# Gated attention of a two-block model: decayed scores and values split for three of four key blocks, products one step later

## The chip, the cores and the metric

One core of one Trainium2 chip. The metric is the device time of one execution in microseconds (us), the median of the runs of a kernel. One execution was also recorded by the hardware profiler; its rows are in microseconds unless marked ns.

## The reference

The model is two transformer blocks over 512 tokens of width 1024. The change lies in the first block's gated attention (4 heads of 128), which the reference computes in chunks with a running state. Cut to one chunk:

```python
sc = jnp.einsum('bhtd,bhsd->bhts', qc, kc) * jnp.exp(dmat - m_t[..., None])
...
num = (jnp.einsum('bhts,bhse->bhte', sc, vc)
       + w_inter[..., None] * jnp.einsum('bhtd,bhde->bhte', qc, C))
den = sc.sum(axis=-1) + w_inter * jnp.einsum('bhtd,bhd->bht', qc, n)
h = num / jnp.maximum(jnp.abs(den), jnp.exp(-m_t))[..., None]
```

Behind it come a norm over each head, `hb * rsqrt(mean(hb * hb) + eps)`, a gain and a gate `sigmoid(ob)`.

## The kernel before

**Number format.** Where the kernel wants accuracy and speed, it splits an f32 tile x into a high part (x copied to F32R) and a low part (x minus the high part) and multiplies in three F32R passes, `split_mm` (L471 to L475): high by high, high by low, low by high. Where it does not split, it multiplies f32 by f32 in one instruction pair, which TensorE runs more slowly.

**Weights.** They stream through a ring of three slots: the SP queue loads a unit (128 x 1024), ScalarE makes `w_hi` (`feed`, L1122), GpSimd makes `w_lo` (`low_part`, L417), TensorE multiplies. A unit of a gate is one output tile of 512 tokens over 8 inner tiles, so 24 passes of 512 columns. `quarter(name, q)` issues a quarter of a unit (6 passes), and the code puts quarters between the steps of an attention so that TensorE has work while the other engines prepare.

**The gated attention.** The whole of it is computed as one masked product over 512 tokens, key block by key block (i = 0 to 3, of 128 keys). Only queries from i * 128 on see block i, so its width is 512, 384, 256 and 128 columns. For each head h and block i:
- ScalarE makes the decay (`decay`, L1363 and L1365: Relu, then Exp) in `em[i % 2]`.
- TensorE makes the scores S (L797) in bank 2 or 3.
- VectorE masks the diagonal part of the decay (L2056) and multiplies scores by decay into `em[2 + i % 2]` (L2060); this frees the bank and counts `ml_sc`.
- TensorE multiplies the values (L806, bank 4) and ones (L807, bank 5: the denominators) by that tile, summing over the blocks, and counts `ml_nd`. Both are f32. These are called P0 to P3 below.

Then VectorE finishes the head: a copy of a gate tile (L1861), two operations on the denominators (L2074, L2075), a reciprocal (L2078) and the multiply L2079; ScalarE squares the result (L1438), TensorE sums the squares (`mean_square`, L786), ScalarE takes the norm (`head_rms`, L1410 and L1413), VectorE applies it (`head_y`, L2039 and L2041), ScalarE and VectorE split it (`head_out` L1417, `head_low` L2046).

**The order of the work is written out by hand** for each engine. Before the change TensorE's order in head h is: quarter 0, S0, quarter 1, the squares' sum of head h-1, S1, P0, quarter 2, S2, P1, quarter 3, S3, P2, quarter 4, P3, quarters 5, 6, 7. VectorE has, for block i, the mask and the multiply, and puts `head_y(h-1)` behind block 1 and `head_low(h-1)` behind block 2 (in head 0 the last rotary tile, `rope(7)`, behind block 1). ScalarE has in head h: a feed of a weight unit, `head_rms(h-1)`, decay 2, `head_out(h-1)`, decay 3, a feed, an Exp for the floor of the denominator, decays 0 and 1 of head h+1, and the square. Ahead of head 0, ScalarE has the eighth copy of the rotary stage (L1393) with four DMA issues (L1398).

Behind the four heads stands the next attention (`softmax_attention`, scores L654), whose first softmax on VectorE is queued behind the last head's L2079.

Of the kernel before, what the change touches and what calls it, by code (L numbers as in the profile page):

```python
# [20 lines left out]
F32 = mybir.dt.float32  # L21
F32R = mybir.dt.float32r
# [4 lines left out]
P = 128  # L27
T = 512
# [88 lines left out]
def build(nc, stream, xT, memT, vecs, tabs, relb, outT):  # L117
    with ExitStack() as ctx, ExitStack() as work:
# [69 lines left out]
        em = [ar(f"em{i}", [P, T], F32, 72 + 2 * i) for i in range(4)]  # L188
        mprobs = [ar(f"mprobs{i}", [P, T], F32, 56 + 2 * i) for i in range(4)]
# [270 lines left out]
        def _(pe):  # L460
# [261 lines left out]
            def first_unit(j, order):  # L722

                for k2, i in order:
# [6 lines left out]
                    pe.wait_ge(named("first_lo"), k + 1)  # L731
# [56 lines left out]
            for h in range(NHB):  # L788
                quarter("gate1a", 8 * h)
                for i in range(QT + 1):  # L790
                    if i < QT:
                        b = 2 + i % 2
                        acquire(b)
                        if h == 0 and i == 0:
                            pe.wait_ge(named("qkb_done"), 8)
                            pe.wait_ge(named("vb_copied"), 4)
                        pe.matmul(ps[:, b, 0:T - i * P], qkb[:, 4 + h, i * P:i * P + P], qkb[:, h, i * P:T],  # L797
                                  start=True, stop=True).then_inc(named("ml_s"), 1)
                    if i >= 1:
                        j = i - 1  # L800
                        if j == 0:
                            acquire(4)
                            acquire(5)
                        pe.wait_ge(named("ml_sc"), QT * h + i)
                        x = em[2 + j % 2][:, 0:T - j * P]
                        pe.matmul(ps[:, 4, j * P:T], vb[:, j, h * P:h * P + P], x, start=j == 0, stop=j == QT - 1)  # L806
                        pe.matmul(ps[:, 5, j * P:T], ones, x, start=j == 0, stop=j == QT - 1)\  # L807
                          .then_inc(named("ml_nd"), 1)
                    if i < QT:
                        quarter("gate1a", 8 * h + 1 + i)  # L810
                    if i == 0 and h >= 1:
                        mean_square(h - 1)
                for q in range(QT + 1, 8):
                    quarter("gate1a", 8 * h + q)
# [292 lines left out]
        def _(act):  # L1107
# [151 lines left out]
            def first_raw(k):  # L1259

                if f"x{k}" in loads:
                    act.wait_ge(loads[f"x{k}"], 16)
                act.activation(first_hi[:, k], hT[:, k], ACT.Copy, scale=vec[:, VEC["mix"] + k:VEC["mix"] + k + 1])\
                   .then_inc(named("first_hi"), 1)
# [142 lines left out]

            def head_rms(h):
# [10 lines left out]
            for h in range(NHB):  # L1419
                feed_after(FIRST["gate1a"] + 2 * h)  # L1420
                if h >= 1:
                    head_rms(h - 1)
                decay(h, 2)
                if h >= 1:
                    head_out(h - 1)
                decay(h, 3)
# [385 lines left out]
        def _(dve):  # L1812
# [107 lines left out]
            def first_low(k):  # L1920

                dve.wait_ge(named("first_hi"), k + 1)
                dve.scalar_tensor_tensor(out=first_lo[:, k], in0=hT[:, k], scalar=v("mix", k),
                                         in1=first_hi[:, k].bitcast(F32), op0=ALU.mult, op1=ALU.subtract)\
                   .then_inc(named("first_lo"), 1)
# [109 lines left out]

            def head_y(h):
# [12 lines left out]
            for h in range(NHB):  # L2049
                for i in range(QT):  # L2050
# [7 lines left out]
                    if QT * h + i >= 2:  # L2058
                        dve.wait_ge(named("ml_nd"), QT * h + i - 1)
# [3 lines left out]

                    if i == 1 and h >= 1:
                        head_y(h - 1)
# [570 lines left out]
```

## Time and profile before

| | |
|---|---|
| median of 3 runs | 1717.01 us (1716.93 to 1717.64) |
| profiled execution, its own time | 1717.28 us |
| its span | 1715.5 us |
| TensorE busy | 1702.6 us (99%) |
| VectorE, ScalarE, GpSimd busy | 859.4, 650.1, 657.6 us |
| granted TensorE clock | 0.999 |
| w_lo on GpSimd (L417) | x261, mean 2471 ns |
| w_hi on ScalarE (L1122) | x272, mean 1055 ns |

The span runs from the first to the last recorded instruction; the profiled execution's own time is 1.8 us longer. A matmul's record covers its whole way through the array and overlaps the next one, so its price is read from start to start. An f32 matmul leaves two records, each with a weight load of its own.

### The profile page before, as it was taken

What the parts mean: (1) busy time and instruction counts of PE and PEld (TensorE: products, weight loads), DVE (VectorE), ACT (ScalarE), POOL (GpSimd) and SP (SyncE); (2) the same over time, 40 slices, a digit from 0 to 9 for tenths busy, and PEclk for the clock granted to TensorE, in tenths of its full rate; (3) what the DMA queues carried; (4) which work ended last, traced back from release to release, by engine and by line L of the source; (5) the groups of instructions that cost most, each with busy time, mean ns of one, the idle gap of its engine ahead of it and who ended that gap; (6) DMA issues with size and microseconds to landing.
All of it is one profiled execution on the core that took longest, in us unless ns stands there. A gap on an engine that the chain in (4) does not pass through costs nothing.

```text
span 1715.5 us, 23737 instructions
## 1 busy us (share of the span) xinstructions
PE 1702.6 (99%) x8133; PEld 1362.2 (79%) x8133; DVE 859.4 (50%) x1398; ACT 650.1 (38%) x1076; POOL 657.6 (38%) x276
## 2 busy tenths in 40 slices
PE   9999999999999999999999999999999999999998
PEld 6888676788888888888688766778888988888887
DVE  5733665574655552208387675551333775555013
ACT  6333444534222222327433576452223522222122
POOL 2443322244544444444333100224444344444443
PEclk9999999999999999999999999999999999999999
DMA  5354211223332333224422111122333233333331
GB/s 188 105 190 129 92 62 50 74 74 123 111 98 94 92 96 104 90 99 129 145 85 88 37 50 45 55 59 93 95 98 98 84 101 98 98 95 93 105 96 64
DMA packets 47635, 162.29 MB, mean 95 GB/s; under 512 B 5724, under 2 KB 7900, under 8 KB 47304
## 3 DMA queue, kind: packets, MB, share of 16 engines
q1 hardware_dynamic: 43872, 151.10, 27.9%
q10 hardware_dynamic: 3688, 10.20, 1.9%
q8 instruction: 46, 0.75, 0.2%
q14 instruction: 29, 0.24, 0.0%
HBM read 156.91 MB, written 4.76 MB: 94 GB/s over the span
## 4 chain that ended last, share of the span: by engine, by line
PE 94%; DVE 2%; ACT 1%; issue 1%; DMA 1%; ACTq 0%; SPq 0%; DVEq 0%
PE ps L473 27%; PE ps L475 27%; PE ps L474 27%; PE ps L672 2%; PE ps L654 2%; PE ps L1052 1%; PE ps L1051 1%; PE ps L1053 1%; PE ps L698 1%; PE ps L911 1%; PE ps L952 1%; PE ps L881 1%; PE ps L933 1%; DVE tmp L1825 1%; PE ps L680 0%
## 5 line engine op out<-in xcount | busy, mean ns | idle before, releaser
L417 POOL TENSOR_TENSOR w_lo<-w_raw,w_hi 128x1024 fp32r<-128x1024 f32 x261 | 644.5, 2471 | 1038.5 <-ACT w_hi L1122 1011.6
L473 PE MATMUL ps<-u_hi,w_hi 128*128 128x512 f32 x1352 | 545.8, 404 | 0.2
L475 PE MATMUL ps<-u_hi,w_lo 128*128 128x512 f32 x1352 | 527.5, 390 | 0.0
L474 PE MATMUL ps<-u_lo,w_hi 128*128 128x512 f32 x1352 | 526.7, 390 | 0.0
L1122 ACT ACTIVATE w_hi<-w_raw 128x1024 fp32r<-128x1024 f32 x272 | 286.6, 1055 | 398.8 <-PE ps L475 331.8
L473 PEld LDWEIGHTS ps<-u_hi,w_hi 128*128 128x128 f32 x1352 | 254.0, 188 | 61.1 <-issue 10.6
L475 PEld LDWEIGHTS ps<-u_hi,w_lo 128*128 128x128 f32 x1352 | 253.7, 188 | 53.8
L474 PEld LDWEIGHTS ps<-u_lo,w_hi 128*128 128x128 f32 x1352 | 254.3, 188 | 51.6 <-issue 2.4
L1519 ACT ACTIVATE tmp<-tmp 128x512 f32<-128x512 f32 x44 | 27.8, 632 | 213.2 <-DVEq L2169 213.2
L2179 DVE TENSOR_TENSOR a_lo<-tmp,a_hi 128x512 f32 (+1 forms) x44 | 105.3, 2392 | 5.6 <-DVE a_hi L2178 1.6
L473 PE MATMUL ps<-a_hi,w_hi 128*128 (+1 forms) x264 | 102.9, 390 | 0.0
L475 PE MATMUL ps<-a_hi,w_lo 128*128 (+1 forms) x264 | 102.7, 389 | 0.0
L474 PE MATMUL ps<-a_lo,w_hi 128*128 (+1 forms) x264 | 102.7, 389 | 0.0
L2175 DVE TENSOR_TENSOR tmp<-ps,tmp 128x512 f32<-128x512 f32 x44 | 30.4, 692 | 91.5 <-PE ps L475 91.2
L2167 DVE TENSOR_TENSOR tmp<-ps,tmp 128x512 f32<-128x512 f32 x44 | 30.4, 692 | 58.6 <-PE ps L475 45.0
L473 PEld LDWEIGHTS ps<-a_hi,w_hi 128*128 128x128 f32 x264 | 49.6, 188 | 10.5
L475 PEld LDWEIGHTS ps<-a_hi,w_lo 128*128 128x128 f32 x264 | 49.6, 188 | 10.4
L474 PEld LDWEIGHTS ps<-a_lo,w_hi 128*128 128x128 f32 x264 | 49.6, 188 | 10.1
L2136 DVE TENSOR_TENSOR tmp<-ps,tmp 128x512 f32<-128x512 f32 x16 | 11.1, 692 | 91.1 <-PE ps L475 90.0
L473 PE MATMUL ps<-m_hi,w_hi 128*128 128x512 f32 (+1 forms) x152 | 54.3, 357 | 0.0
L475 PE MATMUL ps<-m_hi,w_lo 128*128 128x512 f32 (+1 forms) x152 | 54.1, 356 | 0.0
L474 PE MATMUL ps<-m_lo,w_hi 128*128 128x512 f32 (+1 forms) x152 | 54.0, 356 | 0.0
(373 smaller groups left out, 2398.1 us busy)
## 6 DMA issues: line engine op xcount, KB each, us to landing
w_raw<-stream SPq DMA_DIRECT2D x277, 512.0 KB, 3.5
g_rep<-g_one ACTq DMA_DIRECT2D x1, 2560.0 KB, 13.8
spread<-m_rows ACTq DMA_DIRECT2D x4, 512.0 KB, 5.0
tmp<-tmp ACTq DMA_DIRECT2D x32, 64.0 KB, 3.3
bias<-g_rep ACTq DMA_DIRECT2D x1, 2048.0 KB, 10.4
outT<-hT SPq DMA_DIRECT2D x16, 128.0 KB, 1.8
hT<-xT SPq DMA_DIRECT2D x3, 512.0 KB, 7.9
mem_in<-memT ACTq DMA_DIRECT2D x1, 1024.0 KB, 4.7
```

The costliest lines, as they stand in the source:

```text
L417: pool.tensor_tensor(w_lo[:, slot], w_raw[:, slot], w_hi[:, slot].bitcast(F32), ALU.subtract)\
L473: pe.matmul(out, wh, xh, start=start, stop=False)
L474: pe.matmul(out, wh, xl, start=False, stop=False)
L475: return pe.matmul(out, wl, xh, start=False, stop=stop)
L654: m = pe.matmul(ps[:, 2 + e, 0:keys[t]], head_q(h, t), head_k(h, keys[t]), start=True, stop=not extra(t))
L672: m = pe.matmul(ps[p0:p1, b, t * P:t * P + P], values(h, kb), prT[e][:, kb * P:kb * P + P], start=kb == 0, stop=kb == nb - 1)
L698: m = pe.transpose(ps[:, 4 + e, kb * P:kb * P + P], pr[s % 4][:, kb * P:kb * P + P], ident)
L1122: act.activation(w_hi[:, slot], w_raw[:, slot], ACT.Copy).then_inc(hi_ready, 1)
L1519: act.activation(tmp[0][:, :], tmp[1][:, :], ACT.Sigmoid).then_inc(named(name + "_e"), 1)
L2167: step(dve.tensor_tensor(tmp[1][:, :], ps[:, banks[0], :], tmp[3][:, :], ALU.mult))
L2175: step(dve.tensor_tensor(tmp[4][:, :], ps[:, banks[1], :], tmp[2][:, :], ALU.mult))
L2179: step(dve.tensor_tensor(a_lo[:, bass.ds(k, 1)], a, a_hi[:, bass.ds(k, 1)].bitcast(F32), ALU.subtract))
```

## The change

The decayed scores of blocks 0 to 2 are copied to a high part by ScalarE (`em_high`) and the low part is made by VectorE (`em_low`). The values of key blocks 0 to 2 are split once for all heads (`vb_hi` on ScalarE, `vb_lo` on VectorE, written over the f32 values), and ScalarE makes an F32R copy of the ones. For these blocks TensorE issues three F32R passes for the values and two for the ones; block 3 stays f32. In the loop over steps, the products of block j come at step j + 2, not j + 1, so P0 stands behind S2, P3 behind quarter 5, and quarters 6 and 7 are left behind it. `em_low(h, i-1)` stands on VectorE behind the multiply of block i. On ScalarE, `head_rms` and `head_out` come behind `em_high` of blocks 0 and 1. The semaphores `first_hi` and `first_lo` get other names and count these parts too.

```diff
@@ -186,6 +186,11 @@
         g1b = [ar(f"g1b{k}", [P, T], F32, 40 + 2 * k) for k in range(KT)]
         rows = ar("rows", [4, 8, T], F32, 56)
         em = [ar(f"em{i}", [P, T], F32, 72 + 2 * i) for i in range(4)]
+        vb_hi = ar("vb_hi", [P, QT - 1, T], F32R, 56)
+        vb_lo = ar("vb_lo", [P, QT - 1, T], F32R, 40)
+        em_hi = [ar(f"em_hi{i}", [P, T], F32R, 64 + 2 * i) for i in range(2)]
+        em_lo = [ar(f"em_lo{i}", [P, T], F32R, 68 + 2 * i) for i in range(2)]
+        ones_r = ar("ones_r", [P, P], F32R, 88)
         mprobs = [ar(f"mprobs{i}", [P, T], F32, 56 + 2 * i) for i in range(4)]
         mprobsT = [ar(f"mprobsT{i}", [P, T], F32, 64 + 2 * i) for i in range(2)]
         cos = ar("cos", [P, T], F32, 90)
@@ -787,31 +792,37 @@
 
             for h in range(NHB):
                 quarter("gate1a", 8 * h)
-                for i in range(QT + 1):
+                for i in range(QT + 2):
                     if i < QT:
                         b = 2 + i % 2
                         acquire(b)
                         if h == 0 and i == 0:
                             pe.wait_ge(named("qkb_done"), 8)
-                            pe.wait_ge(named("vb_copied"), 4)
                         pe.matmul(ps[:, b, 0:T - i * P], qkb[:, 4 + h, i * P:i * P + P], qkb[:, h, i * P:T],
                                   start=True, stop=True).then_inc(named("ml_s"), 1)
-                    if i >= 1:
-                        j = i - 1
+                    if i >= 2:
+                        j = i - 2
                         if j == 0:
                             acquire(4)
                             acquire(5)
-                        pe.wait_ge(named("ml_sc"), QT * h + i)
-                        x = em[2 + j % 2][:, 0:T - j * P]
-                        pe.matmul(ps[:, 4, j * P:T], vb[:, j, h * P:h * P + P], x, start=j == 0, stop=j == QT - 1)
-                        pe.matmul(ps[:, 5, j * P:T], ones, x, start=j == 0, stop=j == QT - 1)\
-                          .then_inc(named("ml_nd"), 1)
-                    if i < QT:
-                        quarter("gate1a", 8 * h + 1 + i)
+                        c = slice(h * P, h * P + P)
+                        if j < QT - 1:
+                            pe.wait_ge(named("lo_parts"), KT + QT - 1 + (QT - 1) * h + j + 1)
+                            xh, xl = em_hi[j % 2][:, 0:T - j * P], em_lo[j % 2][:, 0:T - j * P]
+                            split_mm(ps[:, 4, j * P:T], vb_hi[:, j, c], vb_lo[:, j, c], xh, xl, j == 0, False)
+                            pe.matmul(ps[:, 5, j * P:T], ones_r[:, :], xh, start=j == 0, stop=False)
+                            pe.matmul(ps[:, 5, j * P:T], ones_r[:, :], xl, start=False, stop=False)\
+                              .then_inc(named("ml_nd"), 1)
+                        else:
+                            pe.wait_ge(named("vb_copied"), 4)
+                            pe.wait_ge(named("ml_sc"), QT * (h + 1))
+                            x = em[2 + j % 2][:, 0:T - j * P]
+                            pe.matmul(ps[:, 4, j * P:T], vb[:, j, c], x, start=False, stop=True)
+                            pe.matmul(ps[:, 5, j * P:T], ones, x, start=False, stop=True).then_inc(named("ml_nd"), 1)
+                    quarter("gate1a", 8 * h + 1 + i)
                     if i == 0 and h >= 1:
                         mean_square(h - 1)
-                for q in range(QT + 1, 8):
-                    quarter("gate1a", 8 * h + q)
+                quarter("gate1a", 8 * h + 7)
 
             softmax_attention(
                 "moba", A_STEPS, hq(qa), hk(ka), KEYS, lambda h, kb: va[:, kb, h * DA:h * DA + DA],
@@ -1405,6 +1416,20 @@
                     decay(0, 0)
                     decay(0, 1)
 
+            act.activation(ones_r[:, :], ones, ACT.Copy).then_inc(named("vb_copied"), 1)
+            for j in range(QT - 1):
+                act.activation(vb_hi[:, j], vb[:, j], ACT.Copy).then_inc(named("vb_copied"), 1)
+
+            def em_high(h, i):
+
+                n = T - i * P
+                act.wait_ge(named("ml_sc"), QT * h + i + 1)
+                if i == 2:
+                    act.wait_ge(named("ml_nd"), QT * h + 1)
+                elif h >= 1:
+                    act.wait_ge(named("ml_nd"), QT * (h - 1) + (3 if i == 0 else 2))
+                act.activation(em_hi[i % 2][:, 0:n], em[2 + i % 2][:, 0:n], ACT.Copy).then_inc(named("hi_parts"), 1)
+
             def head_rms(h):
                 act.wait_ge(named("ml_ms"), h + 1)
                 own.step(act.activation(tmp[3][:, :], ps[:, RMS_BANK, :], ACT.Ln, scale=1.0 / DB,
@@ -1418,12 +1443,15 @@
 
             for h in range(NHB):
                 feed_after(FIRST["gate1a"] + 2 * h)
+                em_high(h, 0)
+                decay(h, 2)
                 if h >= 1:
                     head_rms(h - 1)
-                decay(h, 2)
+                em_high(h, 1)
+                decay(h, 3)
                 if h >= 1:
                     head_out(h - 1)
-                decay(h, 3)
+                em_high(h, 2)
                 feed_after(FIRST["gate1a"] + 2 * h + 1)
                 if h == 0:
                     act.wait_ge(named("rope_done"), 7)
@@ -2033,6 +2061,18 @@
             dve.wait_ge(named("sob_done"), 4)
             dve.wait_ge(named("upto_in"), 1)
 
+            for j in range(QT - 1):
+                dve.wait_ge(named("vb_copied"), 4 + 1 + j + 1)
+                dve.tensor_tensor(vb_lo[:, j], vb[:, j], vb_hi[:, j].bitcast(F32), ALU.subtract)\
+                   .then_inc(named("lo_parts"), 1)
+
+            def em_low(h, i):
+
+                n = T - i * P
+                dve.wait_ge(named("hi_parts"), KT + (QT - 1) * h + i + 1)
+                dve.tensor_tensor(em_lo[i % 2][:, 0:n], em[2 + i % 2][:, 0:n], em_hi[i % 2][:, 0:n].bitcast(F32),
+                                  ALU.subtract).then_inc(named("lo_parts"), 1)
+
             def head_y(h):
 
                 dve.wait_ge(named("ml_rs"), h + 1)
@@ -2055,12 +2095,14 @@
                     dve.wait_ge(named("ml_w"), QT * h + i + 1)
                     step(dve.tensor_tensor(w[:, 0:P], upto_ps, w[:, 0:P], ALU.mult))
                     dve.wait_ge(named("ml_s"), QT * h + i + 1)
-                    if QT * h + i >= 2:
-                        dve.wait_ge(named("ml_nd"), QT * h + i - 1)
+                    if h >= 1 and i == 1:
+                        dve.wait_ge(named("ml_nd"), QT * h)
                     step(dve.tensor_tensor(em[2 + i % 2][:, 0:n], ps[:, 2 + i % 2, 0:n], w[:, 0:n], ALU.mult))
                     dve.sem_inc(bank_free[2 + i % 2], 1)
                     dve.sem_inc(named("ml_sc"), 1)
 
+                    if i >= 1:
+                        em_low(h, i - 1)
                     if i == 1 and h >= 1:
                         head_y(h - 1)
                     if i == 2 and h >= 1:
```

## Rows read from the trace of the kernel before

**Rows 1.** The page, busy us (share of the span) and instructions of TensorE.

```profile
PE 1702.6 (99%) x8133; PEld 1362.2 (79%) x8133; DVE 859.4 (50%) x1398; ACT 650.1 (38%) x1076; POOL 657.6 (38%) x276
```

**Rows 2.** Windows, one head: us, busy of each engine, granted clock, DMA.

```profile
189.10:207.63 18.53, 18.53 (x75) 13.31 (x74) 12.54 (x18) 8.91 (x15) 4.76 (x2) 1.00 0.28 86
```

**Rows 3.** Timeline, TensorE, second head: start us, us, engine, line, operation.

```profile
193.90 1.02 PE L807 MATMUL ps<-em,kept 128*128 128x512 f32 x2
...
196.14 0.59 PE L797 MATMUL ps<-qkb 128*128 128x256 f32 x2
196.57 0.81 PE L806 MATMUL ps<-em,vb 128*128 128x384 f32 x2
197.21 0.81 PE L807 MATMUL ps<-em,kept 128*128 128x384 f32 x2
...
199.46 0.60 PE L806 MATMUL ps<-em,vb 128*128 128x256 f32 x2
199.89 0.59 PE L807 MATMUL ps<-em,kept 128*128 128x256 f32 x2
...
201.93 0.39 PE L807 MATMUL ps<-em,kept 128*128 128x128 f32 x2
...
209.88 1.10 PE L786 MATMUL ps<-tmp,kept 128*128 128x512 f32 x2
```

**Rows 4.** Timeline, TensorE, third attention of the second block: one-pass products.

```profile
1000.84 0.39 PE L475 MATMUL ps<-u_hi,w_lo 128*128 128x512 f32 x1
1001.07 0.28 PE L927 MATMUL ps<-soft_hi,negtri_r 128*128 128x256 f32 x1
1001.18 0.28 PE L929 MATMUL ps<-soft_lo,negtri_r 128*128 128x256 f32 x1
1001.30 0.39 PE L933 MATMUL ps<-tmp,kept 128*128 128x128 f32 x2
```

**Rows 5.** Timeline, VectorE, second head into the third, and the last.

```profile
202.41 0.69 DVE L1861 COPY g1a<-ps 128x512 f32<-128x512 f32 x1 [2.40 <-PE ps L807]
...
208.29 0.69 DVE L2079 TENSOR_TENSOR tmp<-ps,tmp 128x512 f32<-128x512 f32 x1
...
210.49 0.69 DVE L2060 TENSOR_TENSOR em<-ps,em 128x512 f32<-128x512 f32 x1
...
212.56 1.18 DVE L2039 SCALAR_TENSOR_TENSOR tmp<-tmp,vec,tmp 128x512 f32<-128x512 f32 x1 [0.25 <-ACT tmp L1413]
...
252.91 0.75 DVE L2039 SCALAR_TENSOR_TENSOR tmp<-tmp,vec,tmp 128x512 f32<-128x512 f32 x1 [0.99 <-ACT tmp L1413]
```

**Rows 6.** Timeline, ScalarE, the same stretch.

```profile
209.18 0.63 ACT L1438 ACTIVATE tmp<-tmp 128x512 f32<-128x512 f32 x1 [5.11 <-DVEq L2081]
...
211.02 0.69 ACT L1410 ACTIVATE tmp<-ps,small 128x512 f32<-128x512 f32 x1 [0.27 <-PE ps L786]
...
212.37 0.49 ACT L1363 ACTIVATE em<-spread,acol 128x256 f32<-128x256 f32 x1
212.89 0.42 ACT L1365 ACTIVATE em<-em 128x256 f32<-128x256 f32 x1
```

**Rows 7.** Timeline, ScalarE and VectorE, start of the first head.

```profile
174.67 1.06 ACT L1122 ACTIVATE w_hi<-w_raw 128x1024 fp32r<-128x1024 f32 x1 [2.72 <-issue]
...
172.00 0.69 DVE L2060 TENSOR_TENSOR em<-ps,em 128x512 f32<-128x512 f32 x1 [0.49 <-PE ps L797]
```

**Rows 8.** Timeline of GpSimd; groups by line and form; one tile, ns min/median/max.

```profile
210.83 2.36 POOL L417 TENSOR_TENSOR w_lo<-w_raw,w_hi 128x1024 fp32r<-128x1024 f32 x1 [7.80 <-ACT w_hi L1122]
...
L2179 DVE TENSOR_TENSOR a_lo<-tmp,a_hi 128x512 f32 x36 | 93.5, 2597 | 5.3 <-DVE a_hi L2178 1.6
...
L2321 DVE TENSOR_TENSOR soft_lo<-tmp,soft_hi x16: 424/558/694, 975.8 to 1057.7; 128x256 fp32r<-128x256 f32 x8, 128x512 fp32r<-128x512 f32 x8
```

**Rows 9.** Timeline, TensorE, second step of the next attention.

```profile
248.18 0.70 PE L654 MATMUL ps<-ka,qa 64*128 64x256 f32 x4
```

**Rows 10.** Line L741, 3.6 to 4.4: duration ns min/median/max.

```profile
L741 PE MATMUL ps<-blank x4: 379/467/634, 3.3 to 4.3; 128*128 128x512 bf16 x4
```

More of the change, by code:

```diff
@@ L730, in first_unit @@
                         pe.wait_ge(lo_ready, j + 1)
-                    pe.wait_ge(named("first_lo"), k + 1)
+                    pe.wait_ge(named("lo_parts"), k + 1)
                     m = split_mm(ps[:, VB_BANKS[i], :], first_hi[:, k, x], first_lo[:, k, x],
@@ L1263, in first_raw @@
                 act.activation(first_hi[:, k], hT[:, k], ACT.Copy, scale=vec[:, VEC["mix"] + k:VEC["mix"] + k + 1])\
-                   .then_inc(named("first_hi"), 1)
+                   .then_inc(named("hi_parts"), 1)
             def first_square(k):
@@ L1920, in first_low @@
             def first_low(k):
-                dve.wait_ge(named("first_hi"), k + 1)
+                dve.wait_ge(named("hi_parts"), k + 1)
                 dve.scalar_tensor_tensor(out=first_lo[:, k], in0=hT[:, k], scalar=v("mix", k),
                                          in1=first_hi[:, k].bitcast(F32), op0=ALU.mult, op1=ALU.subtract)\
-                   .then_inc(named("first_lo"), 1)
+                   .then_inc(named("lo_parts"), 1)
             def first_add(k):
@@ L2034, in _ @@
             dve.wait_ge(named("upto_in"), 1)
+            for j in range(QT - 1):
+                dve.wait_ge(named("vb_copied"), 4 + 1 + j + 1)
+                dve.tensor_tensor(vb_lo[:, j], vb[:, j], vb_hi[:, j].bitcast(F32), ALU.subtract)\
+                   .then_inc(named("lo_parts"), 1)
+            def em_low(h, i):
[3 more added lines that the diff above has]
+                                  ALU.subtract).then_inc(named("lo_parts"), 1)
             def head_y(h):
```

## The prediction

> **What bounds the kernel.** I read the page first: TensorE is busy 1702.6 of 1715.5 us [rows 1], so nearly every microsecond that another engine costs TensorE here comes out at the end, and nearly every one it saves too. Then the windows by stage: one head of the gated attention, 189.10 to 207.63, is 18.53 us with TensorE busy throughout at the full granted clock [rows 2]. Then the timeline of that head on TensorE [rows 3], where the start of one instruction to the start of the next is its real price, since the recorded durations overlap. Last the VectorE and ScalarE timelines from one head to the next [rows 5, 6], because the change lays its new work there and moves the products. About 0.2% (3.4 us) is what a measurement of this kernel can tell from no change.
>
> **What TensorE gains.** An f32 product of 384 columns takes 0.64 us (196.57 to 197.21), one of 256 takes 0.43 (199.46 to 199.89) [rows 3]. A one-pass (F32R) product of 512 columns takes 0.23 (1000.84 to 1001.07) and of 256 columns 0.115 (1001.07 to 1001.30 for two) [rows 4]; for 384 I take the middle, 0.17. So a quarter of a gate unit (6 products of 512) is 1.36. The ones product of 512 columns and the quarter behind it take 193.90 to 196.14, 2.24 [rows 3], less 1.36 is 0.88: 0.85 for the product and 0.03 for the passage from f32 to one-pass.
> - Removed per head: values 0.85 + 0.64 + 0.43 and ones 0.88 + 0.67 + 0.46: 3.93.
> - Added per head: five one-pass products for each of three blocks, 5 x (0.23 + 0.17 + 0.115) = 2.58, and 0.03 three times: 2.68.
> - Saved: 1.25 per head, 5.0 over four heads. The fourth block (128 columns) stays f32.
>
> Bounds of this term: if the 384-column product cost as much as the 512, 0.3 less per head (3.8 in all); if the ideal halves and quarters held, 5.4.
>
> **What is in the way of it.** Four places, worked out as a schedule with the rows' own durations: 0.2 us from VectorE to TensorE or ScalarE, 0.25 from TensorE to VectorE. The same schedule laid out for the old order gives the old starts (next head, sum of squares, start of the second attention) to within 0.1.
>
> *Before the first head.* In the old order VectorE makes the first decayed scores at 172.00 [rows 7]. Now it first subtracts three vb_lo, which need three vb_hi from ScalarE, and those stand behind ScalarE's last rotary copy and its four DMA issues, so they start when its w_hi does now, 174.67 [rows 7]. ones_r (about 0.2) and three copies at 0.54 apart end at 176.5; w_hi (1.06) moves behind them. VectorE subtracts from 175.6 to 177.7, and em(0) is done at 179.0 instead of 172.7. Queued behind that wait on VectorE is the whole head. TensorE has done two scores and three quarters at 175.2 and needs bank 2 for S2, which em(0) frees: it **waits 4.0**. Then P0 needs em_hi (ScalarE, 179.2 to 179.8) and em_lo (0.69, after em(1), 180.3 to 181.0): waits 1.5. rope(7) with three steps of 0.69 sits between em_lo(0) and em(2), em_lo(1) ends 185.1: P1 waits 1.2.
>
> *The VectorE/GpSimd read.* em_lo reads two tensors in SBUF, as a_lo of L2179 does, and those 36 take 2597 ns on average where soft_lo at 256 to 512 columns takes 424 to 694 [rows 8]. In the rows of the second head: GpSimd's w_lo runs 210.83 to 213.19, VectorE's two-input L2039 starts at 212.56 and lasts 1.18, till 0.55 behind GpSimd's end [rows 5, 8]; the same operation away from a w_lo, for the last head, is 0.75 (252.91) [rows 5]. So an em_lo that starts while a w_lo runs ends 0.4 to 0.55 after it. em_lo(2) starts some 1 us after ScalarE's second w_hi has set a w_lo going (2.4 us): P2 waits 1.2. The Trainium skill (SBUF — State Buffer, Who interferes with whom) says that whichever of the two starts first holds the pair and the other blocks; by it a w_lo that started second would be the one delayed, and as the two starts in the first head are only 0.15 apart in my schedule, that head could come out 1.2 better; no row settles it.
>
> *Between heads.* In the old order three quarters, S0 and one more quarter lie between P3 and the sum of squares L786. They cover VectorE's finish: P3's last product starts 201.93, the copy L1861 202.41, L2079 ends 208.98, the square 209.18 to 209.81, L786 209.88 [rows 3, 5, 6]: 7.95 from P3's ones, and no slack at all. Products one step later take a quarter out of that cover: 0.25 + 3 x 1.36 + 0.88 + 1.36 = 6.57. **L786 waits 1.4** in heads 1 to 3. Call T the end of L2079. em(0) ends at T+2.2 (211.18 [rows 5]), em(1) at T+3.3, em_hi(0) at T+3.0; w_lo runs T+1.85 to T+4.2 [rows 8], so em_lo(0) ends about T+4.8. TensorE reaches P0 at T+4.4 and waits 0.6. On ScalarE, Ln of the norm (211.02 now, T+2.0 [rows 6]) now stands behind em_hi(0) and the decay of block 2 (212.37, then 212.89 for 0.42: 0.94 in all [rows 6]), so it starts at T+3.8, exp ends T+5.2. VectorE waits for it in head_y, with em(2) and em_lo(1) queued behind: em_lo(1) ends T+8.5 and P1 waits 0.8. em_lo(2) meets the second w_lo again: P2 waits 1.2. Sum 4.0 per head, 12.1 over three; nothing hides it, TensorE has no other work placed there.
>
> *The second attention.* L654 at 248.18 [rows 9] starts with a wait of 0.1 (schedule), for the softmax that VectorE could begin only after the last head's L2079. With one quarter fewer behind the last P3 it waits 1.4 to 1.5 more.
>
> **Sum.** Waits 7.9 + 12.1 + 1.5 = 21.5. A restart after a wait leaves the first weight load in the open: 0.1 each, 16 times, 1.6. Off go the old waits, 1.3 as the schedule of the old order gives them (0.7 in the first head, 0.1 to 0.2 at each L786 and at L654), and the gain, 5.0: 21.5 + 1.6 - 1.3 - 5.0 = **+16.8**. The profiled execution took 1717.28, the median is 0.27 below it, so 1717.01 + 16.8 = **1733.8**. Nothing behind the stage gives it back: TensorE is full to the end [rows 1]. Not costed, because hidden: the vb_copied wait for P3 (long met), and the weight ring: each w_lo is ready some 10 us before its unit.
>
> **Rivals.**
> 1. *No wait between em_lo and w_lo*, because the starts fall otherwise. Then the P2 waits go (4 x 1.2), P0's shrink by 0.45, some of which P1 takes: my schedule without that rule gives +11.7, 1728.7. For: em_lo is short, at 256 columns 0.42. Against: 2597 ns at L2179 [rows 8].
> 3. *Only the first head waits*: if ScalarE and VectorE keep ahead in the later heads, 6.7 to 7.9 of waits less 5.0 and 0.6 leave about +2.5, 1719.5. Against: the 7.95 us chain is in every head of the old profile.
> 4. *Faster: the products are covered.* The place is the step from P3 to L786 and the first S2. If em_lo and the finish came early enough for TensorE never to wait, only the gain is left: 1717.0 - 5.0 = 1712.0. It decides from a finish of 6.6 us or less (now 7.95) and a first em(0) before 175 (now 172.7, new 179.0 by the queue). The rows speak against both.
>
> **How the numbers follow.** Forecast (+13 to +20, both readings of the first head in it) 0.64; rival 1, with what else lies between +7 and +13, 0.16; rival 2 0.10; rival 3 0.06; rival 4 0.04. The range reaches from 1 under rival 1 (its gain at the upper bound, 0.4, and a few tenths of restarts) to 2 over rival 2 (the gain at its lower bound, 1.2, and a tenth or two at each wait): 1727.5 to 1739.0. Left out are rivals 3 and 4 and the tails of the others, under 2 in 10. Rival 4 is faster (0.04); rival 3 is within 3.4 us (0.05 of its 0.06); the rest slower, 0.91.
>
> **What would show it.** Right: TensorE's wait of about 4 us before the third score of head 0; L786 waiting over 1 us for the square L1438 three times; each head 21 to 22 us instead of 18.5; em_lo(2) of about 1.5 to 2.5 us instead of 0.42; values and ones of 512 columns 0.23 apart. Wrong: a head of 17.3 us with TensorE busy throughout (rival 4), em_lo never above 0.7 (rival 1), 512-column products 0.43 apart behind the hole (rival 2), or a first wait under 2 us.

## The result, and the profile after

The changed kernel takes 1731.24 us, the median of 6 runs (1730.98 to 1732.33); the kernel before takes 1717.39, the median of its 6. The ratio is 1.0083 (95% interval 1.0072 to 1.0093): 13.9 us slower. The forecast was 1733.8, slower. The profiled execution took 1732.33 with a span of 1730.5, so the accounts below explain +15.0 of span, a microsecond more than the medians differ by. Three executions in the later batches took 2118, 5565 and 6534 us, far from all others of their kernels, and no median or interval here counts them.

From the page of the changed kernel, TensorE's line, which answers to [rows 1]:

```profile
PE 1702.1 (98%) x8137; PEld 1364.4 (79%) x8145; DVE 872.1 (50%) x1413; ACT 656.6 (38%) x1092; POOL 657.4 (38%) x276
```

TensorE is busy for 0.5 us less and idle for 15.5 more (28.4 for 12.9). Its waits from 165 to 275 us show where it is idle in the changed kernel (each line: who waits, for whom, total us, times, longest):

```profile
PE ps L478 <- DVE em_lo L2073: 7.3, 10, 1.1
PE ps L791 <- ACT tmp L1466: 3.6, 3, 1.2
PE ps L801 <- DVEq L2101: 3.2, 1, 3.2
PE ps L659 <- ACT mprobs L1236: 0.7, 1, 0.7
```

They are the places that the prediction names: products behind `em_lo`, the squares' sum (L786 of before, now L791), the third score of the first head, the second attention (L654, now L659). Timeline of TensorE, first head, then the second, changed kernel (last bracket: idle before it and who ended it):

```profile
178.90 1.04 PE L801 MATMUL ps<-qkb 128*128 128x256 f32 x2 [3.17 <-DVEq L2101]
181.00 0.77 PE L478 MATMUL ps<-em_hi,vb_hi 128*128 128x512 f32 x1 [1.05 <-DVE em_lo L2073]
181.57 0.63 PE L479 MATMUL ps<-em_lo,vb_hi 128*128 128x512 f32 x1
181.99 0.63 PE L480 MATMUL ps<-em_hi,vb_lo 128*128 128x512 f32 x1
...
186.03 0.42 PE L478 MATMUL ps<-em_hi,vb_hi 128*128 128x384 f32 x1
...
198.48 1.12 PE L791 MATMUL ps<-tmp,kept 128*128 128x512 f32 x2 [1.20 <-ACT tmp L1466]
...
202.54 0.47 PE L478 MATMUL ps<-em_hi,vb_hi 128*128 128x512 f32 x1 [0.47 <-DVE em_lo L2073]
...
206.06 0.44 PE L478 MATMUL ps<-em_hi,vb_hi 128*128 128x384 f32 x1 [0.56 <-DVE em_lo L2073]
...
209.57 0.39 PE L478 MATMUL ps<-em_hi,vb_hi 128*128 128x256 f32 x1 [0.97 <-DVE em_lo L2073]
```

Two things are to be seen. In the second head there are four waits, in the order of the forecast. In the first head the hole is there, and behind it and the next wait the products stand 0.42 apart (181.57 to 181.99), where one-pass products of 512 columns stand 0.23 apart [rows 4]. The windows of the changed kernel say why (columns as in [rows 2], the granted clock third from the end):

```profile
175.58:178.90 3.32, 0.16 (x1) 0.00 (x0) 2.79 (x5) 2.24 (x4) 1.00 (x1) 1.00 0.49 167
178.90:181.00 2.10, 1.04 (x2) 0.36 (x3) 1.69 (x4) 1.99 (x5) 1.35 (x1) 0.55 0.00 0
181.00:186.03 5.03, 5.03 (x13) 3.97 (x14) 3.31 (x7) 0.89 (x3) 0.00 (x0) 0.51 0.28 106
186.03:194.87 8.84, 8.84 (x47) 7.62 (x46) 4.13 (x6) 3.97 (x6) 2.40 (x1) 1.00 0.39 119
194.87:216.19 21.32, 18.12 (x78) 13.44 (x77) 15.66 (x21) 10.15 (x18) 4.79 (x2) 1.00 0.21 75
```

From the hole's end to 186.03 the granted clock is 0.51 to 0.55 of full, the level of 1.2 GHz, then 2.4 GHz again. The pair of the third score, which starts at the hole's end, already takes 1.04; behind the same hole in a later run, with the clock still up, it takes 0.70. So the clock fell at this hole, before the second wait began. The last line is the second head: 21.32 us, of which TensorE is busy 18.12; before it was 18.53, all busy [rows 2].

VectorE of the changed kernel, start of the first head and the `em_lo` of two heads:

```profile
175.97 1.90 DVE L2066 TENSOR_TENSOR vb_lo<-vb,vb_hi 128x512 fp32r<-128x512 f32 x3 [4.29 <-ACT vb_hi L1421]
...
186.92 0.43 DVE L2073 TENSOR_TENSOR em_lo<-em,em_hi 128x256 fp32r<-128x256 f32 x1 [0.24 <-DVE em L2100]
...
201.17 1.23 DVE L2073 TENSOR_TENSOR em_lo<-em,em_hi 128x512 fp32r<-128x512 f32 x1 [0.24 <-DVE em L2100]
...
207.62 1.89 DVE L2073 TENSOR_TENSOR em_lo<-em,em_hi 128x256 fp32r<-128x256 f32 x1 [0.25 <-DVE em L2100]
```

and GpSimd beside it:

```profile
187.27 2.40 POOL L422 TENSOR_TENSOR w_lo<-w_raw,w_hi 128x1024 fp32r<-128x1024 f32 x1 [7.02 <-ACT w_hi L1133]
199.45 2.39 POOL L422 TENSOR_TENSOR w_lo<-w_raw,w_hi 128x1024 fp32r<-128x1024 f32 x1 [9.78 <-ACT w_hi L1133]
206.84 2.39 POOL L422 TENSOR_TENSOR w_lo<-w_raw,w_hi 128x1024 fp32r<-128x1024 f32 x1 [4.99 <-ACT w_hi L1133]
```

The same `em_lo` of 256 columns takes 0.43 when it starts ahead of a `w_lo` (186.92 before 187.27) and 1.89 when it starts within one (207.62, w_lo from 206.84 to 209.23; it ends 0.28 behind it).

The account by stretches, from TensorE's starts in both traces: up to the first score +0.42; first head 23.57 for 18.22, **+5.35**; heads 2 and 3 21.3 for 18.5, **+2.8** each; the last head up to the second step of the next attention 25.93 for 22.04, **+3.89**. There TensorE is 15.27 late (263.45 for 248.18). The span ends only 15.0 later: 0.25 is given back near 813 us of the kernel before, outside the change.

### The profile page after: what moved, and what is told of

Read it like the earlier page. It is cut to its first block, busy times and chain, and to the rows that moved or that the text cites. A ratio compares the mean times of both kernels' runs of the same rounds, so it can differ in the third digit from the quotient of the medians.

```text
span 1730.5 us, 23798 instructions
## 1 busy us (share of the span) xinstructions
PE 1702.1 (98%) x8137; PEld 1364.4 (79%) x8145; DVE 872.1 (50%) x1413; ACT 656.6 (38%) x1092; POOL 657.4 (38%) x276
## 4 chain that ended last, share of the span: by engine, by line
PE 90%; DVE 6%; ACT 2%; issue 1%; DMA 1%; SPq 0%; ACTq 0%; DVEq 0%
PE ps L478 26%; PE ps L480 26%; PE ps L479 26%; PE ps L677 2%; PE ps L659 2%; PE ps L1064 1%; PE ps L1063 1%; PE ps L1062 1%; PE ps L703 1%; DVE tmp L2120 1%; PE ps L963 1%; PE ps L892 1%; DMA w_raw<-stream 1%; PE ps L922 1%; PE ps L944 1%
```

## The experiments

Medians are compared with the kernel before in the same batch, on the same chip. In the code cuts, `...` stands for lines left out. The changed kernel run again in the last batch:

> The changed kernel without any edit, on the same chip as the two beside it, so that differences of 1 us between them can be read: 1731.2, ratio 1.0083 to the kernel before. A difference over 0.7 us would say that the distance between the two kernels depends on the chip.

1731.62 for 1717.45, ratio 1.0083 (1.0070 to 1.0097): +14.2, where the first comparison gave +13.9.

**One part alone: the products' step** (in the kernel before, f32 kept).

```diff
-                for i in range(QT + 1):
+                for i in range(QT + 2):
...
-                    if i >= 1:
-                        j = i - 1
+                    if i >= 2:
+                        j = i - 2
```

> The kernel before with one part of the change alone: the products come one step later, all still f32, no split. Theory (cover): the finish of a head, 7.95 us from P3 to the sum of squares, loses one quarter of its cover, so TensorE waits 1.2 to 1.45 us ahead of that sum in heads 1 to 3 and as long ahead of the second step of the next attention: +4.7 us over the kernel before, every head 19.8 to 20.0 us instead of 18.5. Rival (depth): a step more between a multiply and its product only gives slack, +0 to +0.5 us.

1721.52, ratio 1.0024 (1.0015 to 1.0034): +4.1. TensorE's waits of this kernel:

```profile
PE ps L786 <- ACT tmp L1436: 3.5, 3, 1.2
PE ps L654 <- ACT mprobs L1223: 1.1, 1, 1.1
```

So the shift alone, with no split in it, costs one wait in each head but the first, behind the finish of the head before, and one at the next attention. The first head gains: it takes 17.51 for 18.22, since its old wait of 0.48 is gone. The clock stays at 1.00.

**The other part alone: the split, at the old step.**

```diff
-                for i in range(QT + 2):
+                for i in range(QT + 1):
...
-                    if i >= 2:
-                        j = i - 2
+                    if i >= 1:
+                        j = i - 1
```

> The changed kernel with the other part alone: split scores and values, but the products at the old step. Theory: each product now waits for the low part, which VectorE makes only behind the next block's multiply: about 7 us in the first head (the values' parts and the rotary tile are ahead of it), 2.4, 1.7 and 1.4 us at P0, P1, P2 of the others, while the wait ahead of the sum of squares goes back to 0.1: +20 to +24 us over the kernel before. So the later step is what makes the split bearable, though it has its own price. Rival: the split alone costs nothing and the loss comes from the later step: -3 to 0 us.

1744.37, ratio 1.016 (1.0143 to 1.0177): +26.9, more than the +20 to +24 expected. Its waits, and its timeline at the first products of the second head:

```profile
PE ps L478 <- DVE em_lo L2075: 23.8, 12, 6.6
```

```profile
206.11 0.48 PE L478 MATMUL ps<-em_hi,vb_hi 128*128 128x512 f32 x1 [2.25 <-DVE em_lo L2075]
206.42 0.40 PE L479 MATMUL ps<-em_lo,vb_hi 128*128 128x512 f32 x1
206.66 0.43 PE L480 MATMUL ps<-em_hi,vb_lo 128*128 128x512 f32 x1
206.89 0.62 PE L813 MATMUL ps<-em_hi,ones_r 128*128 128x512 f32 x1
207.31 0.63 PE L814 MATMUL ps<-em_lo,ones_r 128*128 128x512 f32 x1
```

All twelve splits now stand on TensorE's path, and L791 no longer waits. The later step is thus what makes the split bearable: it takes 23.8 us of waits down to 10.5 (7.3 behind `em_lo`, 3.2 at the third score) and costs some 4. The parts do not add (4 and 27 give 14 together). The surplus over the expectation shows in the timeline: behind the 2.25 us wait the second and the third product stand 0.24 apart, and from 206.89 on they stand 0.42 apart. The clock fell here too, for some 3 us in each of the three later heads (granted clock 0.50 from 206.89 to 210.30), and in the first head for some 10 us, from 176 to 186, in and behind a wait of 6.6.

**The hole of the first head, filled.** 13 one-pass products of other data, overwritten later, keep TensorE at work ahead of the third score. The hole is the only wait that they fill:

```diff
+                        if h == 0 and i == 2:
+                            acquire(4)
+                            for _ in range(13):
+                                pe.matmul(ps[:, 4, :], u_hi[:, 0, 0:P], u_lo[:, 0], start=True, stop=True)
```

> The changed kernel with 13 F32R products of 512 columns of other data into the free bank 4, ahead of the third score of the first head, where TensorE stood still for 3.3 us; their result is overwritten. About 3.0 us of work, so it delays nothing. Theory (the clock fell because of the hole): the granted clock stays at 1.00 through the stretch and the first head's P0 is 0.23 a product again; but the 2.2 us that the eleven half-speed products cost stood partly where P1 and P2 would have waited anyway, so the time falls by only 0 to 1.5 us against the changed kernel (1731.2). Rival 1: the clock falls for another reason (the mix of products) and stays at 0.5 there: no gain, or a loss. Rival 2: the clock's 2.2 us were all on the path: 1729.0.

1731.17 (three executions), ratio 1.0083 (1.0063 to 1.0103): by the medians no change from the changed kernel. The theory of this run, that the clock would stay up, failed. The wait behind the fill remains, and slow products follow it:

```profile
175.22 3.11 PE L801 MATMUL ps<-u_lo,u_hi 128*128 128x512 f32 x13
178.54 0.70 PE L805 MATMUL ps<-qkb 128*128 128x256 f32 x2 [0.22 <-DVEq L2106]
180.64 0.59 PE L478 MATMUL ps<-em_hi,vb_hi 128*128 128x512 f32 x1 [1.40 <-DVE em_lo L2078]
181.03 0.63 PE L479 MATMUL ps<-em_lo,vb_hi 128*128 128x512 f32 x1
181.46 0.63 PE L480 MATMUL ps<-em_hi,vb_lo 128*128 128x512 f32 x1
```

So either of the two waits can bring the clock down without the other: in the changed kernel the hole did, before the second wait began, and here 0.22 and 1.40 us of waiting did. But here the clock fell later, behind the score, and was back at about 184.2, not at 186. That shows in the profile: the first head takes 22.88 (170.94 to 193.82) for 23.57, since fewer products are slow and em_lo(2) still starts ahead of the `w_lo` (185.86 before 186.23). Then both waits were filled, with 14 products and 6 more ahead of P0, overwritten too:

```diff
...
+                            else:
+                                for _ in range(6):
+                                    pe.matmul(ps[:, 4, :], u_hi[:, 0, 0:P], u_lo[:, 0], start=True, stop=True)
```

> Edit: the changed kernel with 14 more one-pass products of 512 columns ahead of the second step of head 0's scores and 6 more ahead of its first products over keys, all into bank 4, which is overwritten. They keep TensorE at work in both waits of the first head (3.2 us and 1.4 us). Theory A, the clock fell for what TensorE stood still in the two waits together and not for either alone: the granted clock stays at 1.00 through the first head, the 11 products behind the second wait come 0.23 us apart instead of 0.43. The time moves little, since the second part of the low split (behind 1.9 us of VectorE's work beside GpSimd) then sets the start of the last head block's products: 1731.2 less 0 to 1.0 us, so 1730.2 to 1731.2. Theory B, the clock's fall is what the first head pays: with the clock at 1.00 the whole 11 x 0.2 = 2.2 us comes back, about 1729.0. Theory C, waits are not what the fall hangs on: the clock falls at about 181 us all the same and the time is 1731.2 or above.

1732.01, ratio 1.0086 (1.0073 to 1.01), beside 1731.62 for the changed kernel in the same batch. Its timeline of TensorE and one row each of VectorE and GpSimd:

```profile
180.63 0.47 PE L478 MATMUL ps<-em_hi,vb_hi 128*128 128x512 f32 x1
180.94 0.40 PE L479 MATMUL ps<-em_lo,vb_hi 128*128 128x512 f32 x1
181.17 0.39 PE L480 MATMUL ps<-em_hi,vb_lo 128*128 128x512 f32 x1
...
184.66 0.45 PE L478 MATMUL ps<-em_hi,vb_hi 128*128 128x384 f32 x1 [1.05 <-DVE em_lo L2081]
...
187.80 0.38 PE L478 MATMUL ps<-em_hi,vb_hi 128*128 128x256 f32 x1 [0.59 <-DVE em_lo L2081]
```

```profile
185.38 2.37 DVE L2081 TENSOR_TENSOR em_lo<-em,em_hi 128x256 fp32r<-128x256 f32 x1 [0.24 <-DVE em L2108]
```

```profile
185.06 2.40 POOL L422 TENSOR_TENSOR w_lo<-w_raw,w_hi 128x1024 fp32r<-128x1024 f32 x1 [5.14 <-ACT w_hi L1141]
```

The clock stays at 1.00 and the products stand 0.23 apart, as expected; the time is above the 1730.2 to 1731.2 expected, and nothing is won: P1 now waits 1.05 and P2 0.59. P1's wait is that for the second `em_lo`, which was there under the slow clock too, hidden behind slower work. P2's comes of the read that VectorE and GpSimd share: with the quarters faster, the `w_lo` now starts at 185.06, ahead of the `em_lo` at 185.38, which takes 2.37 where it took 0.43. Of the 2.2 us that 11 products at 0.2 make up, 0.06 is left: the first head takes 23.51 (170.91 to 194.42) for 23.57, and the medians show nothing. The kernel with one wait filled, whose clock fell for 3.5 us, had the shorter first head.

**The first head as before, the rest as changed.** Its products stay f32 at the old step, the values are split meanwhile:

```diff
-                for i in range(QT + 2):
+                for i in range(QT + (2 if h else 1)):
...
-                    if i >= 2:
-                        j = i - 2
+                    for j in (([], [], [0], [1], [2], [3]) if h else ([], [0], [1], [2], [3]))[i]:
...
-            for j in range(QT - 1):
-                act.activation(vb_hi[:, j], vb[:, j], ACT.Copy).then_inc(named("vb_copied"), 1)
...
+                if h == 0:
+                    feed_after(FIRST["gate1a"])
+                    decay(0, 2)
+                    decay(0, 3)
+                    values_high()
```

> Edit: head 0 of the first block's attention as in the kernel before (float32 products one step earlier, values split into parts meanwhile); heads 1 to 3 as the change has them, nothing moved. Theory A, the costs of the heads stand side by side: heads 1 and 2 cost 2.8 us each and head 3 3.9 us over the kernel before, 9.5 us in all, and the first head's 5.35 us go: 1717.2 + 9.5 = 1726.7, at most 0.5 us less because the values' split is hidden. The clock stays at 1.00 throughout. Rival B, the first head's loss hid part of the later ones' (a queue emptied while it stood), so that they grow when it goes: 1728 to 1731. Rival C, the later heads' waits come from work of the first head that was late: they shrink, below 1725.

1724.85, ratio 1.0044 (1.0031 to 1.0058): +7.4, where the three later heads side by side would give +9.5, and 1.8 below the 1726.7 expected. The waits of this kernel show the reason:

```profile
PE ps L478 <- DVE em_lo L2088: 5.9, 9, 1.0
PE ps L791 <- ACT tmp L1480: 2.4, 2, 1.2
PE ps L659 <- ACT mprobs L1243: 0.7, 1, 0.7
PE ps L811 <- DVEq L2119: 0.4, 1, 0.4
```

L791 waits twice, not three times: the second head takes 19.96 (189.27 to 209.23) and the two behind it 21.33 and 25.62. The wait that stands in head 2 is made by how head 1 ends (two quarters or three behind P3), so it goes with the first head: 1.36 us (19.96 for 21.32). Another 0.3 is gone from P1 of the last head (0.54 for 0.87), for which no cause was looked for. My expectation had booked the wait to the head in which it shows; this is rival C's mechanism, for that one wait.

**The waits of the later heads, one by one.** The second weight feed behind the next head's decays, so that `em_lo(2)` comes before the `w_lo`:

```diff
                 em_high(h, 2)
-                feed_after(FIRST["gate1a"] + 2 * h + 1)
...
+                feed_after(FIRST["gate1a"] + 2 * h + 1)
                 act.wait_ge(named("ml_h"), h + 1)
```

> The changed kernel with ScalarE's second weight copy of each head moved behind the decays of the next head, so that GpSimd's w_lo starts some 3 us later and no longer lies over em_lo of block 2. Theory (the read that VectorE and GpSimd share): em_lo of block 2 falls from 1.9 to 0.43 us in heads 1 and 2 and TensorE's wait of 0.97 ahead of P2 goes there; head 3 has no decays to move behind and keeps or worsens its wait; about -2 us against the changed kernel, 1729.2. Rival: em_lo of block 2 is slow for another reason (its buffer, its width): it stays at 1.9 us and the time at 1731.2.

1730.18 (three executions), ratio 1.0073 (1.0053 to 1.0093), a microsecond above the 1729.2 expected. In the second and third head `em_lo(2)` takes 0.42 and 0.43 for 1.89, P2's wait of 0.97 is gone, and a head takes 20.06; in the last, which has no next head's decays to stand behind, it takes 2.51 and P2 waits 1.73. The medians alone don't part it from the changed kernel (intervals overlap); the rows do. P3 right behind P2, so that three quarters cover the finish again:

```diff
-                    if i >= 2:
-                        j = i - 2
+                    for j in ([], [], [0], [1], [2, 3], [])[i]:
```

> The changed kernel with P3 (the f32 products of block 3) right behind P2 instead of one quarter later, so that quarters 5, 6 and 7 all lie behind it again. Theory (cover): the 1.2 us of wait ahead of the sum of squares falls to 0.1 in heads 1 to 3, and the wait ahead of the next attention's second step with it; nothing else changes: -5.4 us against the changed kernel, 1725.8. Rival: the waits only move to P0 of the next head, whose low part hangs on the same finish: under -2 us.

1726.89, ratio 1.0057 (1.0042 to 1.0073), 1.1 above the 1725.8 expected. No wait is left at L791 and L659, and a head takes 19.93. The norm of the head before one block later, on ScalarE (shown) and in the same way on VectorE (`head_y` behind block 2, `head_low` behind block 3):

```diff
-                if h >= 1:
-                    head_rms(h - 1)
                 em_high(h, 1)
                 decay(h, 3)
                 if h >= 1:
+                    head_rms(h - 1)
+                em_high(h, 2)
+                if h >= 1:
                     head_out(h - 1)
-                em_high(h, 2)
```

> The changed kernel with the norm of the head before moved one block later on both engines: on VectorE head_y behind block 2 and head_low behind block 3, on ScalarE head_rms behind the decay of block 3 and head_out behind em_high of block 2. Theory (queue on VectorE): em(2) and em_lo(1) no longer stand behind the wait for the norm, so the waits ahead of P1 (0.5) and P2 (1.0) go in heads 1 to 3, and each head's finish starts that much earlier: -5 to -6 us against the changed kernel, about 1725.5. Rival: those waits are set by the GpSimd overlap alone, and only the time of the norm moves: under -1.5 us.

1724.74, ratio 1.0045 (1.003 to 1.0061). The waits of P1 and P2 are gone in the later heads, those of L791 stand at 1.19, and a head takes 19.26: this one move takes two waits, since it also brings `em_lo(2)` ahead of the second `w_lo` (204.71 before 205.45 in the second head, 0.43 long).

This kernel also shows what the clock is worth. The move leaves the first head's program as it is in the changed kernel, yet the first head takes 22.68 (170.53 to 193.21) for 23.57:

```profile
180.23 0.77 PE L478 MATMUL ps<-em_hi,vb_hi 128*128 128x512 f32 x1 [1.40 <-DVE em_lo L2073]
...
183.28 0.39 PE L480 MATMUL ps<-u_hi,w_lo 128*128 128x512 f32 x1
183.51 0.39 PE L478 MATMUL ps<-u_hi,w_hi 128*128 128x512 f32 x1
```

The hole before the third score is the same (3.16), but here that score's pair still runs at full clock (0.70), the clock falls only behind it, and from 183.28 on the products stand 0.23 apart again. In the changed kernel they were slow until 185.83, and its second trace has the first head at 23.56. So with the same program the clock is low for some 3.5 us in one execution and some 7 in another, and the shorter time is worth 0.9 us of the first head.

All three moves together:

> The changed kernel with all three moves: P3 behind P2, the norm one block later, the second weight copy later. Theory: the heads 1 to 3 have left only the 0.5 us ahead of P0, 18.0 us each against 18.5 before; the first head keeps its hole: -12 us against the changed kernel, 1719.3, some +2 over the kernel before. Rival: new collisions of w_lo with em_lo take most of it back: above 1722.

1720.0, ratio 1.0018 (1.0009 to 1.0027), its waits:

```profile
PE ps L801 <- DVEq L2100: 3.2, 1, 3.2
PE ps L478 <- DVE em_lo L2072: 2.3, 4, 0.9
```

Heads take 17.9. Left are the first head (23.06) and P0's 0.48 in each later one.

**The gain without the waits.** The three moves, the first head as before with the values split in it, and each head's first feed drawn ahead of the square, so that no `w_lo` runs beside `em_lo(0)`:

```diff
+                if h + 1 < NHB:
+                    feed_after(FIRST["gate1a"] + 2 * h + 2)
                 act.wait_ge(named("ml_h"), h + 1)
```

> The three moves, and the first head left as in the kernel before (f32, old step), with the values split while VectorE and ScalarE are idle in it; the next head's first weight copy goes ahead of the wait for the head's end, so that its w_lo lies under the reciprocal. Theory: no hole, the clock stays, P0 no longer meets a w_lo; heads 1 to 3 at 17.3 to 17.7 us instead of 18.5: -3 us against the kernel before, 1714.2. Rival: values' low parts in the first head delay its finish, or the 1.2 us saved per head are eaten by restarts: within 1 us of the kernel before.

1713.29, the median of 11, ratio **0.9978 (0.9969 to 0.9987)**: 3.75 us faster than the kernel before, 0.9 better than the 1714.2 expected. Windows of two of its heads, its `em_lo` by duration (ns, least, middle, longest), and all its waits in the stage:

```profile
188.74:206.13 17.39, 17.39 (x78) 13.43 (x77) 13.58 (x21) 10.17 (x18) 4.78 (x2) 1.00 0.24 81
206.13:223.51 17.38, 17.38 (x78) 13.44 (x77) 13.57 (x21) 10.17 (x18) 4.79 (x2) 1.00 0.20 61
```

```profile
L2087 DVE TENSOR_TENSOR em_lo<-em,em_hi x9: 425/560/694, 193.7 to 233.6; 128x512 fp32r<-128x512 f32 x3, 128x384 fp32r<-128x384 f32 x3, 128x256 fp32r<-128x256 f32 x3
```

```profile
PE ps L811 <- DVEq L2118: 0.3, 1, 0.3
```

With TensorE busy throughout, as before, a head takes 17.39 for 18.53: the split itself gains 1.14 us per head.

## Why the prediction was right, and where it was off

**The gain.** Forecast 1.25 per head, measured 1.14 in the later heads. Four times that is 4.6, between the bounds given (3.8 to 5.4); the first head's own gain was not measured.

**The waits.** A wait costs more than its row says. In the second head 21.32 - 18.53 + 1.14 = 3.93 are lost, and its rows record 1.20 + 0.47 + 0.56 + 0.97 = 3.20: 0.18 more for each on average. A product is recorded for 0.39 where its price is 0.23, so 0.16 of a wait lies under the record before it. The surplus is not the same for every wait: with P0's alone left, a head takes 17.90 for 17.39, 0.03 more than its row of 0.48. With 0.18 added to each row (us):

| wait | forecast | row | row + 0.18 |
|---|---|---|---|
| first head: third score | 4.0 | 3.17 | 3.35 |
| first head: P0, P1, P2 | 1.5, 1.2, 1.2 | 1.05, none, none | 1.23, 0, 0 |
| L791, three times | 1.4 | 1.20 | 1.38 |
| later heads: P0, P1, P2 | 0.6, 0.8, 1.2 | 0.47, 0.56 (0.87 in the last), 0.97 | 0.65, 0.74 (1.05), 1.15 |
| second attention | 1.5 | 0.70 | 0.88 |
| sum | 21.5 | 14.8 | 17.5 |

The waits of the later heads are right to 0.06 each, but for the last head's P1.

Four terms of the sum were too high:
- The 16 restarts (1.6) were counted on top of waits that already held them: the schedule's waits are the real ones, not the rows'.
- The first head's P1 and P2 (2.4) did not come.
- The wait at the third score was 0.65 too long: the three vb_lo and em(0) took 2.8 us from the first one's start (175.97 to 178.79), not 3.4 (175.6 to 179.0).
- The wait at the second attention was 0.62 too long.

P0's wait in the first head was right. With the third score at full clock its row is 1.40 (the hole filled, the norm moved). In the changed kernel 0.35 of it lies under that score's slow pair, 1.04 for 0.70, so it belongs to the measured waits: 17.85.

Four terms were too low or missing:
- The clock, 11 products at 0.2: 2.2. The forecast had this as a rival.
- The gain was 0.4 smaller.
- The old waits were 0.7 in place of 1.3 (one of 0.5, in the first head, and its 0.18).
- The stage starts 0.4 later than in the trace of before. That has no cause in the change: over the traces of all these kernels the first score starts at 170.5 to 171.3.

The sum with measured terms is 17.85 - 0.7 - 4.6 + 2.2 + 0.4 = +15.15, and at the second attention TensorE is 15.27 late. What the forecast had too high comes to 5.3 us and what it had too low to 3.6. That its total lies only 1.8 above the span's +15.0 is thus in part luck: the waits between the heads were computed rightly, the first head and the second attention were not.

**Rival 2, the clock, held in its fact and not in its price.** One of the prediction's own signs of being wrong did come: products of 512 columns stand 0.42 apart behind the hole. The fall cost 0.2 more for each of 11 products (the durations of the blank products had suggested 0.25), but the total is not the rival's 1736.8. The slow products took the place of waits. With the clock held up by both fills, the P1 wait that I forecast and did not find is there at 1.05 and P2's at 0.59, and the first head is only 0.06 shorter. The price is not nothing either: where the clock was low for some 3.5 us and not 7, with em_lo(2) still ahead of the `w_lo`, the first head was 0.7 to 0.9 shorter. No run here has the clock up and em_lo(2) ahead of the `w_lo`. The Trainium skill (TensorE: Matmul & The Clock Gate, What's actually happening) has the rate halve after TensorE has been idle for a stretch, as a state that recent activity sets. The trace agrees that it halves and returns; it differs in that no single long hole is needed, since 0.22 and 1.40 us sufficed with the hole filled.

**The first head's two readings.** The prediction left open which of `em_lo(2)` and `w_lo` starts first there. In the changed kernel it was `em_lo`, by 0.35 us, and the lower reading held (0.43 and no wait at P2); with both waits filled it was `w_lo`, by 0.32, and the other reading came (2.37). The Trainium skill (SBUF — State Buffer, Who interferes with whom) says that a VectorE instruction with two SBUF inputs and a GpSimd instruction that reads SBUF exclude each other, and that issue order decides which is delayed; the trace agrees, 0.43 for 1.89 and 2.37 at the same 256 columns. The other side of it, a `w_lo` that starts second and is delayed, shows in the kernel with P3 moved: a `w_lo` that starts 0.18 into an em_lo (186.75 for 186.57) takes 2.51 where the others beside it take 2.40.

**Rivals 1, 3, 4.** Rival 1 (no wait between the neighbours) fell: 1.89 for 0.42. Rival 3 (only the first head) fell: the three later ones show 9.5 of the 15, and 7.4 are left with the first head as before. (Its own terms, 6.7 to 7.9 less 5.0 and 0.6, give 1.1 to 2.3, not the 2.5 stated.) Rival 4 (faster) was wrong for this order of work and right as a bound: once the finish is covered and `em_lo` stands clear of `w_lo`, the gain is all that remains. In the first head no run here keeps it.

**Not settled.** With the same program the clock was low for some 3.5 us or some 7; what decides which was not tried. `em_lo(1)` of the first head starts 0.61 us after VectorE's last work, naming `em_hi`, in this and the filled kernels; some 0.4 of it has no cause that the rows name. Nor was it tried whether the first head can be split at a gain when the values are split earlier.

## What to carry to other kernels

A faster format on the full engine is worth its time there (1.14 of 18.5 us a head) only if the work that prepares it stands clear of its path: here TensorE waited 24 us for the preparation at the old place and 10.5 one step later, and not at all in three heads once the norm, the last products and the weight feeds were moved as well and the first head was left unsplit. Moving work later in a loop takes cover away from whatever the tail of the loop was hiding; a wait that shows in one turn is made by how the turn before ends, and is to be booked there. Filling both of TensorE's waits to hold its clock brought 0.06 us, since the next wait was set by another engine and took what the faster products freed. Filling only the first brought 0.7 in the profile, which the medians cannot tell from nothing.

## What the runs showed of the hardware that was not expected

- The granted clock fell to the level of 1.2 GHz behind a hole of 3.17 us, after waits of 0.22 and 1.40 us that followed a filled stretch, and some 0.8 us after the end of a wait of 2.25 us; it did not after single waits of 1.2 us, one per head (shift alone), nor in the later heads of the changed kernel with four waits of 0.47 to 1.20. It stayed low for 3.5 us (180.64 to about 184.2) with the hole filled, for some 7 in the changed kernel, and for some 3.5 with the norm moved, though the first head's program is the same in these two.
- Prices of a one-pass product from start to start: 512 columns 0.23, 384 columns 0.18 (185.12 to 185.30 in the kernel with both waits filled), 256 columns 0.12. The first behind another kind or a wait costs 0.08 to 0.1 more (180.63 to 180.94 is 0.31).
- A `w_lo` of GpSimd that starts within a two-input read of VectorE takes 2.51 for 2.40, and an em_lo that starts within a `w_lo` 1.89 to 2.51 for 0.43.
- Two kernels within 0.5 us of each other by medians can have their waits in quite different places (both waits filled, and the changed kernel): the rows of the stage, not the total, tell which mechanism is at work.
